# Six conditioning jobs moved out of the recurrence's tiles into the stage ahead of them

## The chip, the cores and the metric

The kernel runs on one core of a Trainium2 chip, as one program in which the instructions of each engine are written out in order and tied to one another by semaphores. The engines are TensorE (PE, matmuls into PSUM banks), VectorE (DVE), ScalarE (ACT), GpSimd (POOL) and SyncE (SP, which issues most of the DMAs). The metric is device time in microseconds: 1748.57 us, the median of three runs (1746.95 to 1749.58).

## The reference, cut to what matters

Two blocks are computed on 256 tokens of width 1024, all in fp32. The first begins with a conditioning: six vectors are made from `c`, and three of them (`g1`, `sh2`, `sc2`) are what this change moves.

```python
mod = silu(c) @ ada_w + ada_b                       # 1024 -> 6 * 1024
sh1, sc1, g1, sh2, sc2, g2 = split(mod, 6)
h = rms_norm(x, norm1_g) * (1 + sc1) + sh1
z = h @ w_in
y_fox = fox_mixer(z[..., :FOX_COLS], ...)           # attention, 8 heads
y_rwkv = rwkv7_mixer(z[..., FOX_COLS:], ...)        # recurrence, 8 heads
x = x + g1 * (concat([y_fox, y_rwkv]) @ w_out)
h = rms_norm(x, norm2_g) * (1 + sc2) + sh2
x = x + g2 * moe_ffn(h, ...)

# inside rwkv7_mixer
zr = zr + mu * (shift_prev(zr) - zr)                # token shift
w_log = -softplus(-(w0 + tanh(wd) @ decay_up)) - 0.5
a = sigmoid(a0 + ad @ iclr_up)
g = sigmoid(gd) @ gate_up
# per token: S = S * w + (S a) b^T + v k^T ; out = S r
```

A second block (another mixer, cross attention, a gated FFN) follows the experts; it isn't touched.

## The kernel before, in words

**Jobs.** A *job* is one dense product with 512 columns of a weight matrix. Its weights (2 MB, plus 2 KB of bias) are streamed by SyncE into one of two slots of `ring`, job by job in the order of the list `jobs`; the DMA of a job waits until the job two places before it is done (`w_used`, L670). `dense` and `dense_tile` (L1160 to L1186) do a job on TensorE: eight fp32 matmuls of 128x512 (the trace shows two records for each), one for the bias, and at the end a wait for the job's own last matmul. ScalarE copies the result out of its bank (`lin_copy`, L769; `side_copy`, L821). Results go to banks 0 and 1 in turn; `lin_bank` (L610) gives some outputs bank 2 or 3 instead.

**The conditioning jobs.** Each of the vectors takes two jobs (halves). The left operand is `silu_c`, which is ready from the start, so such a job depends only on its weights and may stand anywhere in TensorE's order. The six of this change are SHIFT2 (`sh2`), GATE1 (`g1`) and SCALE2 (`sc2`), in this order in the job list, after the projections and the `g2` jobs. They are used after the recurrence: `g1` where the output projection is added to `x` (L2233), `sc2` at L2225, `sh2` at L2257.

**The stages around them**, in TensorE's order:
1. Attention, eight heads; the projection of the recurrence and the two `g2` jobs stand between the heads. Meanwhile GpSimd does the token shift of `z_rw` in two halves (L1908 to L1919), each by a DMA and three operations.
2. ScalarE takes tanh and sigmoid of the low-rank columns of `z_rw` (L854 to L856) and signals `rw_tanh`.
3. TensorE transposes these columns (L1286) and does the low-rank products (L1292 to L1301); VectorE adds the biases, and ScalarE takes sigmoids (L859, L861).
4. VectorE makes the key norms (L2107 to L2115); ScalarE takes the square root (`rstd`, L862). Only then does VectorE scale `logw` (L2119), and TensorE makes the cumulative sums (L1303 to L1313). VectorE prepares the four operands `til` (L2121 to L2145).
5. The recurrence, two tiles of 128 tokens, each with: transposes of `til` (L1317), Gram products of each head (L1323 to L1326, L1331), an inverse by seven levels of doubling, and the end of the tile.

**A level** (L1340 to L1362) goes through two groups of four heads. For each group TensorE multiplies by `gram` (L1347), VectorE masks the result (L2174), TensorE multiplies twice more (L1356, L1360), and VectorE adds both results (L2179, L2181). The first level has no L1347, the last no L1360. In levels 1 to 4 a quarter of a job stands between L1347 and L1356: SHIFT2 in the first tile, SCALE2 in the second.

**The end of a tile**: products L1380, L1388, L1396 and L1398, with a copy by ScalarE after each group (L880 to L884). In the first tile the state's products follow (L1405, L1406), and VectorE makes `stateT` of them (L2189). There the two GATE1 jobs stand: the first in two halves between these products, the second behind them.

ScalarE needs a table load (`ACT_TABLE_LOAD`) where the function changes between the families of exp, square root, tanh and sigmoid. Copies need none.

Of the kernel before, what the change touches and what calls it, by code (L numbers as in the profile page):

```python
# [17 lines left out]
ALU = mybir.AluOpType  # L18
# [118 lines left out]
def build(nc, A, consts, out):  # L137
# [22 lines left out]
    with ctx:  # L160
# [25 lines left out]

        SH, SC, GT = range(3)


# [385 lines left out]
        J_IN2 = J_OUT + 2  # L575
        J_ADA2 = (J_SHIFT2, J_SCALE2)
        N_LATE = 4
# [32 lines left out]
        def lin_bank(o):  # L610


            return o % 2 + 2 * (o in [outputs[(j + i, 0)] for j in J_ADA2 for i in range(2)]
                                or o in [outputs[(J_OUT + 1, t)] for t in range(T)])

        def after(j, t=0):

            return outputs[(j, t)] + 1
# [122 lines left out]
        def _(act):  # L741
# [99 lines left out]
            for h in range(HEADS):  # L841
# [8 lines left out]
                if h < len(FOX_FILL):  # L850
                    side_copy(*FOX_FILL[h])
            rstd(fs[:, 6, 0:16], fs[:, 5, 0:16])

            act.wait_ge(lerp_done, 2)  # L854
            act.activation(z_rw[:, :, 1536:1600], z_rw[:, :, 1536:1600], ACT.Tanh)
            act.activation(z_rw[:, :, 1664:1824], z_rw[:, :, 1664:1824], ACT.Sigmoid).then_inc(rw_tanh, 1)  # L856
            for t in range(T):
                act.wait_ge(lora_in, 2 * t + 1)
                act.activation(logw[:, t, :], logw[:, t, :], ACT.Sigmoid).then_inc(rw_sig, 1)  # L859
                act.wait_ge(lora_in, 2 * t + 2)  # L860
                act.activation(iclr[:, t, :], iclr[:, t, :], ACT.Sigmoid).then_inc(rw_sig, 1)  # L861
            rstd(ws[:, 1, :], ws[:, 0, :])  # L862

# [10 lines left out]
            for t in range(T):  # L874

                side_copy(J_ADA2[t], 0)
                side_copy(J_ADA2[t] + 1, 0)

                act.wait_ge(u_mm, 3 * t + 1)
                act.activation(rhs_u[:, 0, :], bank[2][:, :], ACT.Copy).then_inc(u_evac, 1)  # L880
                act.wait_ge(u_mm, 3 * t + 2)
                act.activation(rhs_u[:, 1, :], bank[3][:, :], ACT.Copy).then_inc(u_evac, 1)
                act.wait_ge(u_mm, 3 * t + 3)
                act.activation(y_rw[:, t, :], bank[2][:, :], ACT.Copy).then_inc(u_evac, 1)  # L884
                if t == 0:
                    for h in range(2):
                        lin_copy(J_GATE1 + h, 0, tmp[:, h * BANK:(h + 1) * BANK])
            rstd(ws[:, 1, :], ws[:, 0, :])
# [265 lines left out]
        def _(pe):  # L1154
# [124 lines left out]
            for h in range(HEADS):  # L1279
# [4 lines left out]
                attend(h)  # L1284

            pe.wait_ge(rw_tanh, 1)  # L1286
            for t in range(T):
# [4 lines left out]
            for t in range(T):  # L1292
# [8 lines left out]
                    .then_inc(sc_mm, 1)  # L1301

            for t in range(T):  # L1303
                pe.wait_ge(logw_ready, t + 1)
                pe.matmul(score_bank()[:, :], cst["mid"][:, :], logw[:, t, :], start=True, stop=True)\
                    .then_inc(sc_mm, 1)
# [7 lines left out]
            for t in range(T):  # L1314
# [12 lines left out]
                for g in range(2):  # L1327
# [5 lines left out]
                    mm.then_inc(sc_mm, 1)  # L1333
                pe.wait_ge(lin_evac, after(J_GATE1 + 1 if t else J_GATE + 1))
                if t == 0:
                    pe.wait_ge(pv_evac, 1)
                else:
                    pe.wait_ge(u_evac, 3)

                for level in range(LEVELS):  # L1340
                    for g in range(2):
                        slots = range(4 * g, 4 * g + 4)
                        step = (LEVELS * t + level) * 2 + g
                        if level:
# [4 lines left out]
                            mm.then_inc(wkv_mm, 1)  # L1349
                        if 1 <= level <= 4:  # L1350

                            n = 2 * (level - 1) + g
                            dense_tile(J_ADA2[t] + n // 4, 0, cb, 1, True, part=(n % 4, 4))
                        pe.wait_ge(wkv_w, step + 1)
# [20 lines left out]

                pe.wait_ge(lin_evac, after(J_ADA2[t] + 1))
                with_state(bank[2], AT_)
# [4 lines left out]
                mm.then_inc(u_mm, 1)  # L1382
                if t == 0:
                    dense_tile(J_GATE1, 0, cb, 1, True, part=(0, 2))
                pe.wait_ge(u_evac, 3 * t + 1)
# [3 lines left out]
                mm.then_inc(u_mm, 1)  # L1389
                if t == 0:  # L1390
                    dense_tile(J_GATE1, 0, cb, 1, True, part=(1, 2))
                pe.wait_ge(u_evac, 3 * t + 2)
# [8 lines left out]
                if t == 0:  # L1401
                    b = score_bank()
                    for pair in range(4):
                        c = slice(pair * P, (pair + 1) * P)
                        pe.matmul(b[:, c], til[:, BT_, 0, c], rhs_u[:, 1, c], start=True, stop=False)  # L1405
                        mm = pe.matmul(b[:, c], til[:, KTT_, 0, c], z_rw[:, 0, 1024 + pair * P:1024 + (pair + 1) * P],  # L1406
                                       start=False, stop=True)
                    mm.then_inc(sc_mm, 1)
                    dense(J_GATE1 + 1, cb, 1, True)

# [518 lines left out]
        def _(dve):  # L1929
# [297 lines left out]
            for j in range(2):  # L2227
                for t in range(T):
                    o = outputs[(J_OUT + j, t)]
                    c = slice(j * BANK, (j + 1) * BANK)  # L2230
                    dve.wait_ge(lin_mm, o + 1)

                    dve.tensor_tensor(xn[:, t, c], bank[lin_bank(o)][:, :], tmp[:, c], ALU.mult).then_inc(lin_evac, 1)  # L2233
                    dve.wait_ge(lin_evac, o + 1)
                    link(dve.tensor_tensor(x[:, t, c], x[:, t, c], xn[:, t, c], ALU.add))
# [614 lines left out]
```

## Time and profile before

| | |
|---|---|
| median of three runs | 1748.57 us |
| lowest, highest | 1746.95, 1749.58 us |
| the profiled execution | 1751.06 us |
| its span, first to last instruction | 1749.2 us |
| mean granted TensorE clock | 0.890 |
| attention's end to the output projection | about 260 to 514 us of the span |

The page shows one execution. Busy times of TensorE's matmuls are modelled at their ends, and records overlap a little. `PEclk`, the granted clock, is a share of full speed: 1.00 is 2.4 GHz, 0.50 is 1.2 GHz, and means between come from stretches that hold both. In a timeline, the bracket at a row's end says how long the engine was idle before it, and what released it; `DVEq` or `POOLq` is the engine's own queue.

### The profile page before, as it was taken

How to read it: one execution, taken by the hardware profiler on the slowest of the kernel's cores; microseconds unless marked ns; L12 is line 12 of the kernel's file. 1: busy time of each engine (PE TensorE's matmuls, PEld its weight loads, DVE VectorE, ACT ScalarE, POOL GpSimd, SP SyncE). 2: the span in 40 equal slices, each digit the busy share in tenths (PEclk: the TensorE clock that was granted, in tenths of full speed). 3: DMA queues.
4: the chain of work that ended last, by engine and by line, in shares of the span. 5: the costliest groups of instructions: out<-in, count | busy, mean ns of one | idle time of the engine just before them, and what ended most of it. 6: DMA issues, size and time to landing. Idle time of an engine off the chain costs nothing.

```text
span 1749.2 us, 17988 instructions
## 1 busy us (share of the span) xinstructions
PE 1482.3 (85%) x6888; PEld 911.6 (52%) x6888; DVE 667.5 (38%) x1195; ACT 360.2 (21%) x605; POOL 34.8 (2%) x20
## 2 busy tenths in 40 slices
PE   6784984698987899999999999589978677599996
PEld 2342441666764444444444444366656436299974
DVE  1201527642454622222222222453355522457652
ACT  0010212000001112222222222134321111334342
POOL 0000032000000000000000000000000000000000
PEclk9888985699987899999999999789858887699998
DMA  7543170022119079999999998644321121145541
GB/s 266 194 153 111 45 217 1 1 97 97 51 47 377 16 316 420 415 421 416 408 420 415 414 414 353 230 133 144 82 63 48 49 96 48 48 145 169 169 169 72
DMA packets 106416, 338.98 MB, mean 194 GB/s; under 512 B 12455, under 2 KB 38474, under 8 KB 80636
## 3 DMA queue, kind: packets, MB, share of 16 engines
q1 hardware_dynamic: 93208, 319.09, 47.7%
q10 hardware_dynamic: 8500, 15.72, 3.2%
q0 software_dynamic: 4656, 3.44, 0.8%
q8 instruction: 37, 0.61, 0.1%
q14 instruction: 15, 0.12, 0.0%
HBM read 333.21 MB, written 1.05 MB: 191 GB/s over the span
## 4 chain that ended last, share of the span: by engine, by line
PE 74%; DVE 12%; another core or an unknown queue 4%; DMA 3%; issue 2%; ACT 2%; POOL 1%; ACTq 1%; DVEq 0%; SPq 0%; PEldq 0%; POOLq 0%
PE bank L1537 13%; PE bank L1171 12%; PE bank L1553 7%; PE bank L1190 5%; PE bank L1191 5%; PE bank L1192 5%; PE bank L1202 2%; PE bank L1500 2%; PE bank L1356 2%; PE bank L1501 2%; PE bank L1518 2%; PE bank L1520 2%; PE bank L1651 2%; DMA ring<-in_ada_b 1%
## 5 line engine op out<-in xcount | busy, mean ns | idle before, releaser
L1171 PE MATMUL bank<-ring,xT 128*128 128x512 f32 (+3 forms) x480 | 200.9, 574 | 18.4 <-DMA ring<-in_w_in 13.0
L1171 PEld LDWEIGHTS bank<-ring,xT 128*128 128x128 f32 x480 | 93.5, 210 | 116.7 <-issue 94.9
L1553 PE MATMUL bank<-dn,tmp 128*64 128x512 f32 x528 | 120.6, 598 | 0.0
L1190 PE MATMUL bank<-mod,w_high 128*128 128x256 f32 x352 | 100.9, 287 | 11.6 <-PE bank L1192 5.4
L1171 PE MATMUL bank<-ring,silu_c 128*128 128x512 f32 x192 | 91.2, 618 | 18.6 <-DMA ring<-in_ada_b 18.0
L2414 DVE TENSOR_TENSOR xT<-bank,mod 128x512 fp32r<-128x512 f32 x66 | 45.6, 692 | 158.0 <-ACT mod L948 150.7
L1191 PE MATMUL bank<-xT,w_high 128*128 128x256 f32 x352 | 99.1, 282 | 0.0
L1192 PE MATMUL bank<-mod,ring 128*128 128x256 f32 x352 | 98.8, 281 | 0.0
L2407 DVE SCALAR_TENSOR_TENSOR tmp<-silu_c,rc,bank 128x256 f32<-128x256 f32 x33 | 22.6, 684 | 196.7 <-ACT silu_c L935 191.4
L2777 DVE TENSOR_TENSOR ring<-ring,w_high 128x1024 fp32r<-128x1024 f32 x66 | 77.6, 1220 | 26.3 <-ACT w_high L1113 24.7
L1202 PE MATMUL bank<-c_ident,xn 128*128 128x128 f32 x120 | 28.3, 415 | 66.8 <-DVEq L2477 25.4
L1190 PEld LDWEIGHTS bank<-mod,w_high 128*128 128x128 f32 x352 | 67.3, 191 | 15.7 <-issue 15.7
L1113 ACT ACTIVATE w_high<-ring 128x1024 fp32r<-128x1024 f32 x66 | 65.8, 1049 | 30.5 <-DMA ring<-in_w_ffn_out 27.3
L1553 PEld LDWEIGHTS bank<-dn,tmp 128*64 128x64 f32 x528 | 35.0, 136 | 68.3 <-issue 68.3
L1500 PE MATMUL bank<-mod,gains 128*128 128x256 f32 x272 | 70.1, 296 | 0.5 <-ACT gains L916 0.5
L1191 PEld LDWEIGHTS bank<-xT,w_high 128*128 128x128 f32 x352 | 66.6, 189 | 0.0
L1171 PEld LDWEIGHTS bank<-ring,silu_c 128*128 128x128 f32 x192 | 36.4, 200 | 57.9 <-issue 50.8
L1192 PEld LDWEIGHTS bank<-mod,ring 128*128 128x128 f32 x352 | 66.6, 189 | 0.0
L1501 PE MATMUL bank<-mod,xn 128*128 128x256 f32 x272 | 66.3, 282 | 0.0
L948 ACT ACTIVATE mod<-bank 128x512 fp32r<-128x512 f32 x64 | 38.2, 597 | 133.8 <-PE bank L1553 133.8
L1500 PEld LDWEIGHTS bank<-mod,gains 128*128 128x128 f32 x272 | 51.5, 189 | 26.9 <-issue 26.2
L1537 PE MATMUL bank<-ring,gains 128*64 128x512 f32 x272 | 62.1, 598 | 1.4 <-ACT gains L922 1.4
(571 smaller groups left out, 2494.9 us busy)
## 6 DMA issues: line engine op xcount, KB each, us to landing
dn<-in_exp_w_down SPq DMA_DIRECT2D x66, 1024.0 KB, 10.5
ring<-in_exp_w_gate SPq DMA_DIRECT2D x34, 1024.0 KB, 9.5
ring<-in_exp_w_up SPq DMA_DIRECT2D x34, 1024.0 KB, 11.6
gu_odd<-in_exp_w_gate SPq DMA_DIRECT2D x32, 1024.0 KB, 10.2
gu_odd<-in_exp_w_up SPq DMA_DIRECT2D x32, 1024.0 KB, 12.3
ring<-in_ada_w SPq DMA_DIRECT2D x12, 2048.0 KB
ring<-in_w_ffn_in SPq DMA_DIRECT2D x22, 1024.0 KB, 5.1
ring<-in_w_in SPq DMA_DIRECT2D x7, 2048.0 KB
```

What stands on the lines that cost most here:

```text
L1113: act.activation(of_unit(w_high, u, q, PIECE), of_unit(ring, u, q, PIECE), ACT.Copy)\
L1171: mm = pe.matmul(bank[lin_bank(o)][:, 0:n], lhs(k, t), ring[:, j % RING, k * n:(k + 1) * n], start=(k == 0), stop=(k == kt - 1 and not bias))
L1190: pe.matmul(out, w[0], x[0], start=start, stop=False, skip_group_check=True)
L1191: pe.matmul(out, w[0], x[1], start=False, stop=False, skip_group_check=True)
L1192: return pe.matmul(out, w[1], x[0], start=False, stop=stop, skip_group_check=True)
L1202: mm = pe.transpose(bank[4 + n % 2][0:rows, lo:hi], src, cst["ident"][0:m, 0:m])
L1500: pe.matmul(out_k, xn_high[:, t, k * P:(k + 1) * P], pick[:, t, :], start=(t == 0), stop=False)
L1501: mm = pe.matmul(out_k, xn_low[:, t, k * P:(k + 1) * P], pick[:, t, :], start=False, stop=(t == T - 1))
L1537: mm = pe.matmul(bank[4][CHUNKS[c], :], hg_k[:, CHUNKS[c]], gate_up_of(gu_w(c), k), start=(k == 0), stop=(k == KT - 1))
L1553: mm = pe.matmul(bank[6 + h][CHUNKS[c], :], act_eT[:, 0, k, CHUNKS[c]], dn[:, 2 * parity + c, lo:lo + BANK], start=(k == 0), stop=(k == D_ ...
L2414: dve.tensor_tensor(y_low[:, c], bank[6 + h][:, :], y_high[:, c].bitcast(F32), ALU.subtract)\
L2777: dve.tensor_tensor(at_piece(w_low), at_piece(ring), at_piece(w_high).bitcast(F32), ALU.subtract)\
```

## The change

Six jobs leave the recurrence. The four of SHIFT2 and GATE1 now stand on TensorE between the attention and the low-rank transposes, and the two of SCALE2 between the low-rank products and the cumulative sums. On ScalarE their copies move too: four ahead of tanh, two ahead of the square root of the key norms. GATE1 is written to a free half of `gain` instead of `tmp`, which the attention still uses; the six jobs now take banks 0 and 1 only. The order of the jobs among themselves, and SyncE's order, stay as they are. The lines of the new kernel are numbered up to 8 off from the old ones.

```diff
+        gate1 = gain[:, 0, :]
...
-            return o % 2 + 2 * (o in [outputs[(j + i, 0)] for j in J_ADA2 for i in range(2)]
-                                or o in [outputs[(J_OUT + 1, t)] for t in range(T)])
+            return o % 2 + 2 * (o in [outputs[(J_OUT + 1, t)] for t in range(T)])
...   # ScalarE
             rstd(fs[:, 6, 0:16], fs[:, 5, 0:16])
+            for h in range(2):
+                side_copy(J_SHIFT2 + h, 0)
+            for h in range(2):
+                lin_copy(J_GATE1 + h, 0, gate1[:, h * BANK:(h + 1) * BANK])
             act.wait_ge(lerp_done, 2)
             act.activation(z_rw[:, :, 1536:1600], z_rw[:, :, 1536:1600], ACT.Tanh)
...
+            for h in range(2):
+                side_copy(J_SCALE2 + h, 0)
             rstd(ws[:, 1, :], ws[:, 0, :])
...
             for t in range(T):
-                side_copy(J_ADA2[t], 0)
-                side_copy(J_ADA2[t] + 1, 0)
...
-                if t == 0:
-                    for h in range(2):
-                        lin_copy(J_GATE1 + h, 0, tmp[:, h * BANK:(h + 1) * BANK])
...   # TensorE
+            for j in range(J_SHIFT2, J_SCALE2):
+                dense(j, cb, 1, True)
             pe.wait_ge(rw_tanh, 1)
...
+            for j in range(J_SCALE2, J_OUT):
+                dense(j, cb, 1, True)
             for t in range(T):
                 pe.wait_ge(logw_ready, t + 1)
...
-                        if 1 <= level <= 4:
-                            n = 2 * (level - 1) + g
-                            dense_tile(J_ADA2[t] + n // 4, 0, cb, 1, True, part=(n % 4, 4))
...
-                if t == 0:
-                    dense_tile(J_GATE1, 0, cb, 1, True, part=(0, 2))
...
-                if t == 0:
-                    dense_tile(J_GATE1, 0, cb, 1, True, part=(1, 2))
...
-                    dense(J_GATE1 + 1, cb, 1, True)
...   # VectorE
-                    dve.tensor_tensor(xn[:, t, c], bank[lin_bank(o)][:, :], tmp[:, c], ALU.mult)
+                    dve.tensor_tensor(xn[:, t, c], bank[lin_bank(o)][:, :], gate1[:, c], ALU.mult)
```

What this does to ScalarE's row of instructions ahead of tanh, before (`mod` and `gain` take the copies of the jobs, `z_rw` holds the low-rank columns, `fs` a small root of the attention):

```order
L767 ACTIVATE fs<-fs 128x16 [waits inv_var]
L855 ACT_TABLE_LOAD
L855 ACTIVATE z_rw<-z_rw 128x2x64 [waits lerp_done]
L856 ACT_TABLE_LOAD
L856 ACTIVATE z_rw<-z_rw 128x2x160
L859 ACTIVATE logw<-logw 128x512 [waits lora_in]
```

The same place in the changed kernel:

```order
L766 ACTIVATE fs<-fs 128x16 [waits inv_var]
L770 ACTIVATE mod<-bank 128x512 [waits lin_mm] x2
L770 ACTIVATE gain<-bank 128x512 [waits lin_mm] x2
L858 ACT_TABLE_LOAD
L858 ACTIVATE z_rw<-z_rw 128x2x64 [waits lerp_done]
L859 ACT_TABLE_LOAD
L859 ACTIVATE z_rw<-z_rw 128x2x160
L862 ACTIVATE logw<-logw 128x512 [waits lora_in]
```

Four copies, each waiting for a job's end, now stand ahead of the table load of tanh.

ScalarE's row between the sigmoids of the second tile and the exponentials of the cumulative sums, before (`ws` is the root of the key norms):

```order
L859 ACTIVATE logw<-logw 128x512 [waits lora_in]
L861 ACTIVATE iclr<-iclr 128x512 [waits lora_in]
L767 ACT_TABLE_LOAD
L767 ACTIVATE ws<-ws 128x16 [waits inv_var]
L866 ACT_TABLE_LOAD
L866 ACTIVATE rhs_u<-bank 128x512 [waits sc_mm]
```

And in the changed kernel:

```order
L862 ACTIVATE logw<-logw 128x512 [waits lora_in]
L864 ACTIVATE iclr<-iclr 128x512 [waits lora_in]
L770 ACTIVATE mod<-bank 128x512 [waits lin_mm] x2
L766 ACT_TABLE_LOAD
L766 ACTIVATE ws<-ws 128x16 [waits inv_var]
L871 ACT_TABLE_LOAD
L871 ACTIVATE rhs_u<-bank 128x512 [waits sc_mm]
```

The two copies of SCALE2 and, behind them, a table load now stand ahead of the root.

TensorE's row in a level of the first tile, one group of heads, before:

```order
L1347 MATMUL bank<-inv,gram 128x128 [waits wkv_upd]
L1347 MATMUL bank<-inv,gram 128x128 x3
L1171 MATMUL bank<-ring,silu_c 128x512 [waits lin_evac,w_full1]
L1171 MATMUL bank<-ring,silu_c 128x512
L1356 MATMUL bank<-invT,amat 128x128 [waits wkv_w]
L1356 MATMUL bank<-invT,amat 128x128 x3
L1360 MATMUL bank<-amat,invT 128x128 x4
```

And in the changed kernel:

```order
L1350 MATMUL bank<-inv,gram 128x128 [waits wkv_upd]
L1350 MATMUL bank<-inv,gram 128x128 x3
L1355 MATMUL bank<-invT,amat 128x128 [waits wkv_w]
L1355 MATMUL bank<-invT,amat 128x128 x3
L1359 MATMUL bank<-amat,invT 128x128 x4
```

The quarter of a job is gone from between the product by `gram` and the product that waits for VectorE's mask (`wkv_w`).

## Rows read from the trace of the kernel before

**Rows 1.** The page, part 1: busy us (share of the span) and instructions, by engine.

```profile
PE 1482.3 (85%) x6888; PEld 911.6 (52%) x6888; DVE 667.5 (38%) x1195; ACT 360.2 (21%) x605; POOL 34.8 (2%) x20
```

**Rows 2.** Timeline, 256 to 282: start, us, engine, line, operation, [idle before <-releaser].

```profile
259.57 0.63 PE L1275 MATMUL bank<-z_fox,xn 128*128 128x64 f32 x2
...
268.36 1.28 ACT L855 ACT_TABLE_LOAD   x1
...
276.38 0.31 ACT L855 ACTIVATE z_rw<-z_rw 128x128 f32<-128x128 f32 x1 [6.74 <-POOLq L1919]
...
278.51 1.54 PE L1202 MATMUL bank<-c_ident,z_rw 128*128 128x128 f32 x6 [18.31 <-ACT z_rw L856]
```

**Rows 3.** Timeline, 290 to 302, VectorE and ScalarE.

```profile
294.94 0.69 DVE L2102 COPY gate<-bank 128x512 f32<-128x512 f32 x1 [3.29 <-PE bank L1300]
...
300.38 0.22 ACT L767 ACTIVATE ws<-ws 128x16 f32<-128x16 f32 x1 [6.62 <-DVE ws L2113]
...
300.63 1.00 DVE L2119 TENSOR_SCALAR logw<-logw 128x512 f32<-128x512 f32 x2 [0.28 <-ACT ws L767]
```

**Rows 4.** Timeline, TensorE: one job alone, and 32 records from 513.86.

```profile
415.01 7.03 PE L1171 MATMUL bank<-ring,silu_c 128*128 128x512 f32 x16
...
423.13 0.60 ACT L771 ACTIVATE tmp<-bank 128x512 f32<-128x512 f32 x1 [8.67 <-PE bank L1176]
...
423.40 1.07 PE L1202 MATMUL bank<-c_ident,til 128*128 128x128 f32 x8 [0.30 <-PE bank L1176]
...
513.86 16.73 PE L1171 MATMUL bank<-ring,xT 128*128 128x512 f32 x32 [0.78 <-DVE xT L1954]
```

**Rows 5.** SyncE's issue of a job's weights, and the stretch after it (columns as rows 8).

```profile
361.55 0.37 SPq L673 DMA_DIRECT2D ring<-in_ada_w  x1
...
361.50:369.50 8.00, 7.92 (x54) 6.60 (x55) 2.55 (x4) 0.56 (x1) 0.00 (x0) 1.00 0.75 261
```

**Rows 6.** Timeline of the first tile's levels: products of the first and fifth to seventh.

```profile
343.59 1.89 PE L1347 MATMUL bank<-inv,gram 128*128 128x128 f32 x8
...
382.46 1.06 PE L1347 MATMUL bank<-inv,gram 128*128 128x128 f32 x8
...
384.84 1.16 PE L1356 MATMUL bank<-invT,amat 128*128 128x128 f32 x8 [1.32 <-DVE amat L2174]
...
390.46 1.06 PE L1347 MATMUL bank<-inv,gram 128*128 128x128 f32 x8
```

**Rows 7.** Timeline of TensorE at the end of each tile.

```profile
397.67 2.00 PE L1380 MATMUL bank<-z_rw,gram 128*128 128x64 f32 x16 [0.84 <-DVEq L2183]
...
409.58 0.41 PE L1396 MATMUL bank<-rhs_u,gram 128*128 128x64 f32 x2
...
413.17 0.44 PE L1405 MATMUL bank<-rhs_u,til 128*128 128x128 f32 x2
...
497.31 1.90 PE L1380 MATMUL bank<-z_rw,gram 128*128 128x64 f32 x16
...
499.89 2.00 PE L1388 MATMUL bank<-rhs_u,invT 128*128 128x64 f32 x16 [0.69 <-ACT rhs_u L880]
```

**Rows 8.** Stretches: their us, busy us by engine (instructions), granted clock, DMA share, GB/s.

```profile
280.00:296.00 16.00, 13.13 (x17) 3.52 (x16) 5.44 (x11) 3.80 (x5) 0.00 (x0) 0.50 0.00 0
304.00:312.00 8.00, 0.71 (x2) 0.00 (x0) 7.62 (x12) 0.37 (x1) 0.00 (x0) 0.71 0.00 0
325.54:337.48 11.94, 11.71 (x76) 11.52 (x77) 5.44 (x9) 0.00 (x0) 0.00 (x0) 0.61 0.00 0
...
384.00:396.00 12.00, 8.27 (x67) 7.70 (x67) 5.62 (x9) 0.00 (x0) 0.00 (x0) 1.00 0.33 125
426.85:435.80 8.95, 8.16 (x77) 7.40 (x78) 5.15 (x8) 0.00 (x0) 0.00 (x0) 1.00 0.41 154
498.00:502.00 4.00, 3.21 (x27) 2.93 (x26) 1.38 (x2) 0.67 (x2) 0.00 (x0) 1.00 0.02 4
504.45:511.17 6.72, 6.72 (x34) 6.72 (x33) 0.00 (x0) 0.00 (x0) 0.00 (x0) 0.50 0.00 0
```

More of the change, by code:

```diff
@@ L575, in build @@
         J_IN2 = J_OUT + 2
-        J_ADA2 = (J_SHIFT2, J_SCALE2)
         N_LATE = 4
@@ L1333, in _ @@
                     mm.then_inc(sc_mm, 1)
-                pe.wait_ge(lin_evac, after(J_GATE1 + 1 if t else J_GATE + 1))
                 if t == 0:
+                    pe.wait_ge(lin_evac, after(J_SCALE2 + 1))
                     pe.wait_ge(pv_evac, 1)
@@ L1374, in with_state @@
                                   start=(pair == 0), stop=False, skip_group_check=True)
-                pe.wait_ge(lin_evac, after(J_ADA2[t] + 1))
                 with_state(bank[2], AT_)
@@ L2231, in _ @@
                     dve.wait_ge(lin_mm, o + 1)
-                    dve.tensor_tensor(xn[:, t, c], bank[lin_bank(o)][:, :], tmp[:, c], ALU.mult).then_inc(lin_evac, 1)
+                    dve.tensor_tensor(xn[:, t, c], bank[lin_bank(o)][:, :], gate1[:, c], ALU.mult).then_inc(lin_evac, 1)
                     dve.wait_ge(lin_evac, o + 1)
```

## The prediction

> **What bounds the kernel now.** I read the page's list of busy times first: TensorE is busy 85% of the span [rows 1], so it sets the time on average. That says nothing about one stage, so I then read the timeline of 256 to 530 us, where all six jobs run before and after the change, and last the granted clock by stretches. In the stage ahead of the recurrence TensorE is not the bound. It ends the attention at 259.57 + 0.63 = 260.20 us and starts the low-rank transposes at 278.51, 18.31 us later, released by ScalarE's sigmoid, which itself ran as soon as GpSimd's token shift was done [rows 2]. After the low-rank products VectorE works alone: its gate copy starts at 294.94, ScalarE gives it the square root at 300.38, and at 300.63 it scales logw for the cumulative sums [rows 3]. In the recurrence TensorE is full as long as it carries pieces of the jobs; in the levels without them it waits for VectorE [rows 6].
>
> **One job.** GATE1's second half runs unbroken at full clock: its matmuls start at 415.01, ScalarE's copy at 423.13 (8.12 us), the next work at 423.40, so a job costs 8.39 us on TensorE while others follow [rows 4]. A burst that starts at half clock pays more: the 32 records from 513.86 last 16.73 us, against 2 x 7.03 = 14.06 for as many at full clock, so about 2.7; I take 3.0, since the job's bias pair is not among them. The weights of a job (2 MB) are issued when the job two places before is done. The load of 361.55 is over inside the 8 us to 369.5, where the engines moved 261 GB/s, 2.1 MB in all [rows 5]. A job lasts 8.39 us, so back-to-back jobs just find their weights. This cover is thin: 1 us more per load would cost up to 1 us at each of the last two jobs of the first group.
>
> **The first group** (SHIFT2, GATE1: four jobs, ahead of the transposes). TensorE: 3 x 8.39 + 8.12 + 3.0 for the half-clock start = 36.3 us. Now the point that decides. ScalarE's four copies stand ahead of its tanh, and the table load of tanh stands behind them (the order rows of the section on the change show it). Before, that load ran at 268.36 under the wait for GpSimd and cost nothing; the step from tanh's start to the transposes was 278.51 - 276.38 = 2.13 us [rows 2]. After, the last copy (0.60), the load (1.28) and that step (2.13) follow the last job: 4.0 us. So the transposes start at 260.20 + 36.3 + 4.0 = 300.5 instead of 278.51: **+22.0 us**. The idle 18.31 us hides two jobs and a little; GpSimd's shift, done by 276.4, is no longer what ends last. Queued behind the waiting tanh are the sigmoids, and for these TensorE, VectorE's loraT copies and everything later. The low-rank products ran at granted clock 0.50 (280 to 296) [rows 8]. TensorE will sit idle for the 4.0 us before them. In 304 to 312, where it is busy for only 0.71 of 8 us, the mean clock is 0.71: it was full in some part and was lost within the stretch [rows 8]. So I give them nothing back: 0, bounds -6.5 (half of their 13.13 busy us) and 0.
>
> **The second group** (SCALE2: two jobs, ahead of the cumulative sums). TensorE: 8.39 + 8.12 + 3.0 = 19.5 us from 294.94 on the old time scale. The sums themselves were needed late, so behind TensorE alone most of this would hide under VectorE's work. But ScalarE's two copies stand ahead of its square root of the key norms, with the table load behind them again, and VectorE waits for that root before it scales logw. So VectorE goes on at 294.94 + 19.5 + 0.60 + 1.28 + 0.25 (300.38 to 300.63) = 316.5 instead of 300.63: **+15.9 us**, on the path, since all that VectorE prepares for the recurrence comes after that wait. The weights are there: they are issued as the GATE1 jobs end.
>
> Sum of costs: 37.9 us. Its bounds are 31 (the low-rank products give back their 6.5) and 43 (loads late, clock slow to rise: some 5 more).
>
> **What the recurrence gives back.** Four levels with pieces take 382.46 - 343.59 = 38.87 us in the first tile. The level after them, without a piece, takes 390.46 - 382.46 = 8.00, and in it TensorE waits 1.32 us for VectorE's mask product [rows 6]. So four bare levels take 32.0, and I add 0.5 because the first products run at half clock. Gain 6.4 a tile, **12.8 us** for both, though the four jobs are 4 x 8.12 = 32.5 us of TensorE time: the rest was already lying in VectorE's shadow. The clock stayed 1.00 in 384 to 396, almost the whole of it bare levels [rows 8], so I expect it to stay there.
>
> End of the first tile: from 397.67 to 423.40 are 25.73 us [rows 7, 4]. Without GATE1 the chain is: first product and ScalarE's copy, 2.58 us (497.31 to 499.89, where the second tile has no filler); the inverse's product and copy, as much; the output products, 413.17 - 409.58 = 3.59; the state's products, 415.01 - 413.17 = 1.84; and 1.0 because VectorE makes the state before it can copy the next transposes. Together 11.6, a gain of 14.1. But in the second tile, where these steps already stand bare, the clock is 1.00 in 498 to 502 and 0.50 in 504.45 to 511.17, and the same output products last 6.72 us [rows 8]. I expect the same in the first tile now: 6.72 for 3.59, 3.68 for 1.84, less 0.5 as VectorE's state is then less late: 16.1, a gain of 9.6. And the second tile's Gram stage, now 8.95 us at 1.00, then goes like the first tile's, 11.94 us at 0.61: 3.0 back. Net **6.6 us**; bounds 6.6 and 14.1.
>
> Here a rule speaks for the change. The Trainium skill (TensorE: Matmul & The Clock Gate, "Why this matters for your kernels") asks for no idle gaps over about 3 us between bursts of matmuls. The gaps here are under 1 us, so by that rule the clock would hold at the end of the tile, and the gain there would be 14.1; the rows of 498 to 511 do not bear it out. It is the first rival.
>
> Another page would make it dearer: the Trainium skill (ScalarE: Activation LUTs, "What ACT_TABLE_LOAD costs") counts a drain of 1.38 us beside each load's 1.28. By it the two loads laid open would add 2.8 us. The trace disagrees: tanh, a load and the sigmoid fit in 2.13 us, so the sum stays.
>
> **Sum.** 22.0 + 15.9 - 12.8 - 6.6 = **+18.5 us**. Against the profiled execution's span of 1749.2 us that is 1767.7, and with the 1.9 us around its span (1751.06 in all) 1769.6; the median of the runs shown, 1748.57, lies 2.5 below that execution, so I forecast **1767 us**. The stages behind only shift: the output projection finds its weights earlier than now, but it never waited for them.
>
> **Rivals.**
> - *The clock holds at the end of the first tile.* Gain there 14.1 instead of 6.6: +11.0, 1759.6 us. For it: small gaps; the clock was 1.00 through all of 384 to 396. Against: the second tile's rows. 15%.
> - *The clock holds everywhere, the change is no slower.* With the long idle stretch filled, TensorE keeps full clock from the first group through the low-rank products and the second group to the Gram products. To the rival above add 6.5 (low-rank products), 3.0 (no second half-clock start), 3.0 (the first Gram stage like the second) and 0.5: +11.0 - 13.0 = -2.0, 1746.6 us. It decides if the clock survives the 4.0 us wait for tanh. Against it stands that it was lost inside 304 to 312. 6%.
> - *VectorE is no bound in the levels.* If bare levels shrank by the jobs' whole time, the levels would give 32.5 instead of 12.8: -1.2, 1747.4 us. The bare level's 8.00 us and its waits stand in the trace, so 2%.
> - *The bare levels lose the clock.* The wide matmuls could be what holds it: 504 to 511 shows that TensorE can be busy 100% and stay at 0.50. TensorE is busy 8.27 of the 12 us from 384 to 396, so 5.5 of a level's 8; at half clock that is 11, and a level about 12 us. For eight levels and the four last ones that is about +47, in all +65, 1814 us; for a part of them +10 to +20 more than forecast. Against: 384 to 396. 7% for all of these.
>
> **Chances and range.** The forecast's own case 70%, with its own range 1760 to 1775: the half-clock starts (1.5 to 5 us each), the loads (up to 2), the tile end. The rest as above. A measurement of this kernel tells 0.2% (3.5 us) from no change. Slower 0.90 (forecast, first rival and lost clock make 0.92; 0.02 goes to what I have not thought of), same 0.05 and faster 0.05 from the second and third rivals, whose times lie close to today's, and that rest. The range 1755 to 1778 holds the forecast's case and the first rival.
>
> **What would show it.** Right: in the profile after, no idle TensorE from 260 to about 296, then some 4 us of it, with tanh's table load inside; transposes near 300; VectorE idle for about 16 us before it scales logw, released by ScalarE's square root, which follows a copy and a table load; levels of 8.0 us in both tiles; the output products of the first tile near 6.7 us at clock 0.50. Wrong: transposes before 295, VectorE not waiting for the root, or levels under 7 us would break the sum; levels of 10 us or more mean that the clock fell there.

## The result and the profile after

| | before | after |
|---|---|---|
| median | 1748.5 us (4 runs, 1746.95 to 1749.58) | 1769.13 us (4 runs, 1766.54 to 1772.84) |
| the profiled execution | 1751.06 us | 1766.78 us |
| its span | 1749.2 us | 1764.9 us |
| mean granted clock | 0.890 | 0.892 |

The ratio of after to before is 1.012, with a 95% interval from 1.0096 to 1.0144: the changed kernel is slower by 20.6 us in the medians. The forecast was 1767 us.

Page of the kernel after, part 1: busy us (share of the span) and instructions, by engine. It answers to [rows 1].

```profile
PE 1493.7 (85%) x6888; PEld 919.1 (52%) x6888; DVE 668.5 (38%) x1195; ACT 360.3 (20%) x605; POOL 34.8 (2%) x20
```

Each engine has as many instructions as before, and the shares hardly moved. Nothing here tells that the kernel became slower, or where; only the timeline does.

Timeline of after, 260 to 302, TensorE (to be read against [rows 2]; columns as there):

```profile
260.95 8.60 PE L1170 MATMUL bank<-ring,silu_c 128*128 128x512 f32 x16
...
270.90 7.10 PE L1170 MATMUL bank<-ring,silu_c 128*128 128x512 f32 x16 [0.30 <-PE bank L1175]
...
287.82 7.10 PE L1170 MATMUL bank<-ring,silu_c 128*128 128x512 f32 x16 [0.30 <-PE bank L1175]
294.85 1.12 PE L1175 MATMUL bank<-ring,ones 1*128 1x512 f32 x2
300.05 1.54 PE L1201 MATMUL bank<-c_ident,z_rw 128*128 128x128 f32 x6 [4.08 <-ACT z_rw L859]
```

And ScalarE in the same stretch:

```profile
296.01 0.60 ACT L770 ACTIVATE gain<-bank 128x512 f32<-128x512 f32 x1 [7.86 <-PE bank L1175]
296.63 1.28 ACT L858 ACT_TABLE_LOAD   x1
297.92 0.31 ACT L858 ACTIVATE z_rw<-z_rw 128x128 f32<-128x128 f32 x1
298.24 1.28 ACT L859 ACT_TABLE_LOAD   x1
299.53 0.47 ACT L859 ACTIVATE z_rw<-z_rw 128x320 f32<-128x320 f32 x1
```

The first group of jobs fills TensorE without a gap for weights (0.30 us between jobs), and the idle time of 18.31 us has become 4.08 us: a copy, a load, tanh, a load, the sigmoid, one behind the other. The transposes start at 300.05 instead of 278.51.

VectorE of after, 316 to 339, around its wait for the root (answers to [rows 3]):

```profile
316.26 0.69 DVE L2095 COPY gate<-bank 128x512 f32<-128x512 f32 x1 [3.29 <-PE bank L1301]
...
321.41 0.25 DVE L2106 RECIPROCAL ws<-ws 128x16 f32<-128x16 f32 x1
337.88 1.00 DVE L2112 TENSOR_SCALAR logw<-logw 128x512 f32<-128x512 f32 x2 [16.22 <-ACT ws L766]
```

ScalarE of after, the work that VectorE waits for:

```profile
327.27 0.60 ACT L770 ACTIVATE mod<-bank 128x512 f32<-128x512 f32 x1 [13.48 <-PE bank L1175]
335.73 0.60 ACT L770 ACTIVATE mod<-bank 128x512 f32<-128x512 f32 x1 [7.86 <-PE bank L1175]
336.34 1.28 ACT L766 ACT_TABLE_LOAD   x1
337.63 0.22 ACT L766 ACTIVATE ws<-ws 128x16 f32<-128x16 f32 x1
```

And TensorE's first SCALE2 job, the longest start of a group in any of the traces (7.03 us at full clock):

```profile
316.15 10.03 PE L1170 MATMUL bank<-ring,silu_c 128*128 128x512 f32 x16
```

VectorE had the input of the root ready at 321.66 and got it at 337.85. The root is 0.22 us of work; what made it late is what stands in front of it on ScalarE.

TensorE of after in the first tile: a bare level, and its end (answers to [rows 6, 7]):

```profile
390.37 1.06 PE L1350 MATMUL bank<-inv,gram 128*128 128x128 f32 x8
392.75 1.16 PE L1355 MATMUL bank<-invT,amat 128*128 128x128 f32 x8 [1.32 <-DVE amat L2167]
...
398.37 1.06 PE L1350 MATMUL bank<-inv,gram 128*128 128x128 f32 x8
...
429.57 2.00 PE L1378 MATMUL bank<-z_rw,gram 128*128 128x64 f32 x16 [0.84 <-DVEq L2176]
432.25 2.00 PE L1384 MATMUL bank<-rhs_u,invT 128*128 128x64 f32 x16 [0.69 <-ACT rhs_u L882]
434.94 0.69 PE L1390 MATMUL bank<-rhs_u,gram 128*128 128x64 f32 x2 [0.69 <-ACT rhs_u L884]
...
441.82 0.74 PE L1399 MATMUL bank<-rhs_u,til 128*128 128x128 f32 x2
...
445.13 1.04 PE L1201 MATMUL bank<-c_ident,til 128*128 128x128 f32 x8
```

The first bare level of the second tile, which began slowly:

```profile
464.93 1.91 PE L1350 MATMUL bank<-inv,gram 128*128 128x128 f32 x8
...
475.41 1.06 PE L1350 MATMUL bank<-inv,gram 128*128 128x128 f32 x8
```

Stretches of after: their us, busy us by engine (instructions), granted clock, DMA share, GB/s.

```profile
300.05:316.20 16.15, 14.60 (x23) 4.57 (x23) 4.64 (x9) 2.52 (x4) 0.00 (x0) 0.50 0.20 77
...
362.80:375.20 12.40, 12.40 (x68) 12.18 (x69) 5.53 (x8) 0.00 (x0) 0.00 (x0) 0.50 0.00 0
384.00:428.00 44.00, 31.93 (x259) 29.84 (x260) 21.16 (x33) 0.00 (x0) 0.00 (x0) 1.00 0.00 1
434.94:441.82 6.88, 6.88 (x33) 6.88 (x33) 0.00 (x0) 0.00 (x0) 0.00 (x0) 0.50 0.00 0
448.80:457.60 8.80, 7.25 (x67) 6.24 (x65) 5.60 (x10) 0.00 (x0) 0.00 (x0) 1.00 0.01 2
461.00:471.00 10.00, 8.34 (x40) 7.81 (x41) 3.83 (x6) 0.00 (x0) 0.00 (x0) 0.55 0.00 0
472.00:512.00 40.00, 29.29 (x238) 27.20 (x236) 19.43 (x31) 0.00 (x0) 0.00 (x0) 1.00 0.00 1
```

A bare level (one without a piece of a job) is 8.00 us, 390.37 to 398.37, with the same 1.32 us wait for VectorE as before the change. The bare levels kept full clock for 44 us with TensorE busy 73% (31.93 of 44). The output products that follow, without any idle time, ran at 0.50. The second tile shows what the prediction did not foresee: its Gram products kept 1.00, and its levels began near 0.5, so that the first took 10.48 us (464.93 to 475.41).

### The profile page after: what moved, and what is told of

Same layout as the page of the kernel before. It is cut to its first block, busy times and chain, and to the rows that moved or that the text cites. A ratio compares the mean times of both kernels' runs of the same rounds, so it can differ in the third digit from the quotient of the medians.

```text
span 1764.9 us, 17987 instructions
## 1 busy us (share of the span) xinstructions
PE 1493.7 (85%) x6888; PEld 919.1 (52%) x6888; DVE 668.5 (38%) x1195; ACT 360.3 (20%) x605; POOL 34.8 (2%) x20
## 4 chain that ended last, share of the span: by engine, by line
PE 75%; DVE 14%; another core or an unknown queue 4%; issue 2%; ACT 2%; DMA 1%; ACTq 1%; DVEq 0%; SPq 0%; PEldq 0%
PE bank L1530 13%; PE bank L1170 13%; PE bank L1546 7%; PE bank L1189 5%; PE bank L1191 5%; PE bank L1190 5%; PE bank L1201 2%; PE bank L1493 2%; PE bank L1355 2%; PE bank L1494 2%; PE bank L1511 2%; PE bank L1513 2%; PE bank L1644 2%; DMA ring<-in_ada_b 1%
## 5 line engine op out<-in xcount | busy, mean ns | idle before, releaser
L1170 PE MATMUL bank<-ring,xT 128*128 128x512 f32 (+3 forms) x480 | 198.7, 569 | 18.3 <-DMA ring<-in_w_in 12.7
L1170 PE MATMUL bank<-ring,silu_c 128*128 128x512 f32 x192 | 94.1, 647 | 19.3 <-DMA ring<-in_ada_b 17.6
## 6 DMA issues: line engine op xcount, KB each, us to landing
dn<-in_exp_w_down SPq DMA_DIRECT2D x66, 1024.0 KB, 10.4
```

The lines of the kernel that those rows point to most:

```text
L1170: mm = pe.matmul(bank[lin_bank(o)][:, 0:n], lhs(k, t), ring[:, j % RING, k * n:(k + 1) * n], start=(k == 0), stop=(k == kt - 1 and not bias))
```

## The experiments

The theory: **ScalarE's order is the price**. The jobs lie in cover, that is in time in which TensorE would wait anyway (for GpSimd's shift, for VectorE's preparations), or are paid back; what is lost is that tanh and the root, short steps that others wait for, stand behind copies that wait for whole jobs. The rival, **the jobs themselves**: TensorE's time ahead of the transposes and sums costs what it costs, wherever the copies stand. Each kernel below was timed beside the kernel before, on the same chip. The first four comparisons share 28 runs of it (median 1750.2) on one chip, the last four 18 (median 1748.01) on another. So a kernel is judged by how far it lies above or below the kernel before of its own comparison: the change is 20.6 us above by the first measurement and 20.5 by its repeat. Of the medians forecast below, three came out 0.3 to 0.8 us under their ranges, and the last two single figures were missed by 2 to 3 us. Lengths between two events of one trace are used where attention ended at different times.

**The root ahead of the SCALE2 copies** (in the kernel after):

```diff
+            rstd(ws[:, 1, :], ws[:, 0, :])
             for h in range(2):
                 side_copy(J_SCALE2 + h, 0)
-            rstd(ws[:, 1, :], ws[:, 0, :])
```

> The changed kernel, with ScalarE's two SCALE2 copies moved behind its square root of the key norms; TensorE's order is untouched. Theory A (ScalarE's order makes the price of the second group): VectorE no longer waits 16.2 us for the root. Its preparation then meets the cumulative sums, which still stand behind the two jobs: about 10 us less than the changed kernel, some 1759 us. Rival B (the two jobs on TensorE ahead of the sums are the price by themselves): the sums can start only about 2.7 us earlier, so 0 to 3 us less, 1766 to 1769 us.

Measured: 1758.85 us (1750.05 to 1762.82, 12 runs), ratio 1.0045 [1.0029 to 1.0061]. It lies 8.7 us above the kernel before instead of 20.6, so 12 us are gone by moving one line. Timeline of this kernel, ScalarE:

```profile
318.32 1.28 ACT L766 ACT_TABLE_LOAD   x1
326.22 0.22 ACT L766 ACTIVATE ws<-ws 128x16 f32<-128x16 f32 x1 [6.62 <-DVE ws L2106]
330.61 0.60 ACT L770 ACTIVATE mod<-bank 128x512 f32<-128x512 f32 x1 [4.17 <-PE bank L1175]
```

And VectorE:

```profile
326.46 1.00 DVE L2112 TENSOR_SCALAR logw<-logw 128x512 f32<-128x512 f32 x2 [0.28 <-ACT ws L766]
...
342.17 0.69 DVE L2130 TENSOR_TENSOR y_rw<-bank,logw 128x512 f32<-128x512 f32 x1 [4.43 <-ACT rhs_u L872]
```

The table load is back under the wait for VectorE, and logw follows the root at once, as before the change. Not all 15.9 us come back: the cumulative sums still stand behind both jobs (339.33 here), and VectorE is idle 4.43 us for them. From the gate copy to the transposes of `til`, where before needs 25.94 us and after 41.87, this kernel needs 30.34 (320.77 to 351.11). So 4.4 us of the second group's price are left with TensorE's order, and 11.5 went with ScalarE's. About 1 us of the 11.5 is the clock: the first of the two jobs took 8.85 us here and 10.03 in after. Against the repeat of after (40.47 us, first job 8.64) it is 10.1.

**Tanh and sigmoid ahead of the first four copies**:

```diff
-            for h in range(2):
-                side_copy(J_SHIFT2 + h, 0)
-            for h in range(2):
-                lin_copy(J_GATE1 + h, 0, gate1[:, h * BANK:(h + 1) * BANK])
             act.wait_ge(lerp_done, 2)
...          # tanh, sigmoid
+            for h in range(2):
+                side_copy(J_SHIFT2 + h, 0)
+            for h in range(2):
+                lin_copy(J_GATE1 + h, 0, gate1[:, h * BANK:(h + 1) * BANK])
```

> The changed kernel, with the four copies of the first group moved behind tanh and sigmoid. The third job then waits for a copy (some 2.5 us), but the 4.1 us idle time of TensorE ahead of the transposes goes. Theory A: 1.5 us less if the clock is lost again before the low-rank products, 8 us less if it holds through them (they run at 0.50 in the changed kernel), 1761 to 1767 us. Rival B (the jobs' own time is all the price): no gain or slower by the 2.5 us.

Measured: 1761.95 us (1760.79 to 1762.95, 6 runs), ratio 1.0069 [1.0050 to 1.0088], 11.7 us above the kernel before instead of 20.6. Timeline of this kernel, TensorE, from the third job to the low-rank products:

```profile
279.79 8.51 PE L1170 MATMUL bank<-ring,silu_c 128*128 128x512 f32 x16 [2.28 <-ACT mod L770]
...
296.69 1.12 PE L1175 MATMUL bank<-ring,ones 1*128 1x512 f32 x2
298.12 0.84 PE L1201 MATMUL bank<-c_ident,z_rw 128*128 128x128 f32 x6 [0.30 <-PE bank L1175]
...
302.86 2.08 PE L1300 MATMUL bank<-gate_up,loraT 128*128 128x512 f32 x2 [0.81 <-DVEq L2088]
```

And stretches of this kernel:

```profile
297.00:299.00 2.00, 1.66 (x8) 0.58 (x6) 0.26 (x1) 0.60 (x1) 0.00 (x0) 1.00 0.02 2
300.00:314.00 14.00, 13.19 (x17) 3.70 (x18) 3.56 (x6) 2.52 (x4) 0.00 (x0) 0.50 0.36 139
```

In this trace the condition of the prediction's second rival (that the clock survives) fails even without the wait. TensorE comes to the transposes at full clock, without the idle 4 us, and does them in 0.84 us instead of 1.54; the low-rank products behind them run at 0.50 all the same. The time from the transposes' start to the gate copy is 15.78 us (298.12 to 313.90) against 16.21 in after. So here it was not the gap that took the clock; the last section shows an execution in which it held for most of this stage.

The gain in the medians is 8.9 us. The traces locate less: from attention's end to the transposes behind the recurrence it is 4.0 against after (268.35 to 264.37) and 1.8 against the repeat of after (266.17). Of the 4.0, only 0.7 lie ahead of the transposes, since the third job now waits 2.28 us for its bank behind the copies that wait behind the sigmoid; 0.4 are in the low-rank products, 1.4 in the second group, whose first job took 8.60 us instead of 10.03, and 1.4 in the first tile. Theory A gave 1.5 us for a clock that is lost, as it was here, so the median stands in its range by luck, and most of this gain has no place in a trace.

**Both edits together**:

> Both orders of the two runs before in one kernel. Theory A: the sum of the two, 12 to 18 us less than the changed kernel, 1751 to 1757 us, close to the kernel before with all six jobs still in the stage ahead. Rival B: 0 to 3 us less.

Measured: 1750.52 us (1741.69 to 1756.49, 12 runs), ratio 0.9992 [0.9972 to 1.0012]. TensorE's third job, and VectorE behind the root:

```profile
281.02 7.11 PE L1170 MATMUL bank<-ring,silu_c 128*128 128x512 f32 x16 [0.44 <-ACT mod L770]
...
319.00 1.00 DVE L2112 TENSOR_SCALAR logw<-logw 128x512 f32<-128x512 f32 x2 [0.28 <-ACT ws L766]
```

With the six jobs where the change put them, and only ScalarE's order mended, the kernel can't be told from the one before: 0.3 us above it instead of 20.6. The two edits alone give 12.0 and 8.9. The rival is refuted as an explanation of the loss. In the traces the stretch from attention's end to the transposes behind the recurrence falls from 268.35 to 250.77 us (before: 250.96). Of these 17.6 us, 3.1 lie ahead of the low-rank transposes, where attention ended 2.2 us later than in the trace of tanh and sigmoid alone and the third job waits only 0.44 us; 11.2 lie in the second group. The other 3.3 stand where no edit was made: 2.3 in the second tile, whose four bare levels took 31.4 us instead of 34.5 because the clock held, and 1.0 in the low-rank products and the first tile. What stays true of the rival: the jobs' time on TensorE (17.5 us more ahead of the transposes, 4.7 more in the second group) is about what the recurrence gives back (21.4), so the move as such gains nothing.

**SCALE2 back in the second tile's levels**, the other four jobs as in after:

```diff
-            for j in range(J_SCALE2, J_OUT):
-                dense(j, cb, 1, True)
...
+                        if t and 1 <= level <= 4:
+                            n = 2 * (level - 1) + g
+                            dense_tile(J_SCALE2 + n // 4, 0, cb, 1, True, part=(n % 4, 4))
```

> The changed kernel with the SCALE2 pair back in the second tile's levels 1 to 4; SHIFT2 and GATE1 stay in the first group. Theory A: the second group's 15.8 us go, and the levels of the second tile give back 5 to 7 us, since there the jobs lie mostly in VectorE's shadow: 9 to 11 us less than the changed kernel, 1758 to 1760 us. Rival B (a job costs TensorE's time wherever it stands): no difference.

Measured: 1757.69 us (1749.92 to 1760.5, 11 runs), ratio 1.0032 [1.0015 to 1.0049]. The logw scaling follows the gate copy by 5.7 us again (315.88, 321.56), and the four levels with pieces take 40.0 us (447.48 to 487.49) against 34.5 in after (464.93 to 499.39). It lies 7.5 us above the kernel before instead of 20.6, so 13.1 are gone. In the traces the second group gives 15.9 and the levels take 5.6, 10.4 net; by the prediction's terms it was 15.9 - 6.4 = 9.5. That a job costs its time wherever it stands is refuted.

**The kernel after, once more**, for its scatter:

> The changed kernel itself, timed beside the next three on one chip: 1.2% above the kernel before by the first measurement (1769 against 1748.5 us). Both theories expect that again; it is the base for the others.

Measured: 1768.53 us (1762.1 to 1772.57, 6 runs), ratio 1.0115 [1.0094 to 1.0136]. The profiled execution shows the same events: transposes at 299.88 after 4.08 us of idle time, VectorE's wait for the root 14.83 us instead of 16.22, because the first SCALE2 job took 8.64 us and not 10.03. The second group cost 14.5 us here (40.47 less 25.94), not 15.9. The second tile's levels again began slowly, 461.95 to 468.23 for the first group of heads, as in after (464.93 to 471.20). The four levels took 34.5 us in four of the five traces that have them bare in the second tile; only in that of both edits, 31.4.

**Only SHIFT2 moved into the gap**, from the kernel before, its copies behind the sigmoid. GATE1 keeps its place in this run and the next, but is written to `gain` as in after:

```diff
             act.activation(z_rw[:, :, 1664:1824], z_rw[:, :, 1664:1824], ACT.Sigmoid).then_inc(rw_tanh, 1)
+            for h in range(2):
+                side_copy(J_SHIFT2 + h, 0)
...
+            for j in range(J_SHIFT2, J_GATE1):
+                dense(j, cb, 1, True)
             pe.wait_ge(rw_tanh, 1)
...
-                        if 1 <= level <= 4:
+                        if t and 1 <= level <= 4:
```

> The kernel before with only the SHIFT2 pair moved, to the place between attention and low-rank transposes, its copies behind tanh and sigmoid. Theory A: two jobs take 19.5 us from the attention's end, 18.3 of which TensorE idles through anyway, so +1.3 us; the first tile's levels give back 6.9. In sum some 5.5 us less than the kernel before, about 1743 to 1745 us. Rival B (levels cannot give back anything since VectorE bounds them, or a moved job costs its time): 1749 us or more.

Measured: 1742.19 us (1736.7 to 1747.51, 12 runs), ratio 0.9961 [0.9947 to 0.9975]. Timeline of this kernel, TensorE:

```profile
260.44 8.92 PE L1172 MATMUL bank<-ring,silu_c 128*128 128x512 f32 x16
...
270.72 7.10 PE L1172 MATMUL bank<-ring,silu_c 128*128 128x512 f32 x16 [0.30 <-PE bank L1177]
277.76 1.12 PE L1177 MATMUL bank<-ring,ones 1*128 1x512 f32 x2
279.18 0.85 PE L1203 MATMUL bank<-c_ident,z_rw 128*128 128x128 f32 x6 [0.30 <-ACT z_rw L856]
```

Attention ends at 260.65 here and the transposes start 18.5 us later, against 18.3 in before: two jobs lie wholly in the wait for GpSimd, whose end they just reach. The first tile's four levels shrink to 32.2 us (341.08 to 373.28), from 38.87. So the bare levels of a tile are worth what the prediction said, and whether a job's move wins depends on the cover at the place where it goes and on what waits behind its copies. The stretch from attention's end to the transposes behind the recurrence is 9.8 us shorter in this trace (250.96 to 241.19), more than the 5.8 of the medians: 3.0 of it is the first Gram stage (22.71 to 19.72), which ran at 0.94 here.

**Only SHIFT2 moved ahead of the sums**, its copies ahead of the root. The matmuls stand before the wait for `logw_ready`:

```diff
+            for h in range(2):
+                side_copy(J_SHIFT2 + h, 0)
             rstd(ws[:, 1, :], ws[:, 0, :])
...
+            for j in range(J_SHIFT2, J_GATE1):
+                dense(j, cb, 1, True)
             for t in range(T):
                 pe.wait_ge(logw_ready, t + 1)
```

> The kernel before with only the SHIFT2 pair moved, to the place ahead of the cumulative sums, its copies ahead of the square root as in the changed kernel's second group. It measures that group's price alone. Theory A: +15.9 us, less 6.9 from the first tile's levels: +9, about 1758 us. Rival B (the price is hidden under VectorE's preparation, as the sums are needed 11 us later than they are made): no change or up to 5 us less, 1744 to 1749 us.

Measured: 1755.25 us (1751.27 to 1758.3, 7 runs), ratio 1.0036 [1.0023 to 1.0049]. VectorE of this kernel, which waits 15.28 us for the root:

```profile
314.87 1.00 DVE L2123 TENSOR_SCALAR logw<-logw 128x512 f32<-128x512 f32 x2 [15.28 <-ACT ws L767]
```

It lies 7.2 us above the kernel before; the same two jobs that save 6 us in the gap cost 7 here. From the gate copy (294.18) to the transposes of `til` (335.11) are 40.93 us, 15.0 more than before. The second group's price is a property of this place and of ScalarE's order, not of what stands ahead of it. This run doesn't separate the two; the first experiment does (4.4 us for the place, the rest for the order).

**Each pair where it finds cover**: SHIFT2 in the gap as above; GATE1 behind the cumulative sums, with its copies behind the exponentials; SCALE2 left in the second tile.

```diff
+            for j in range(J_GATE1, J_SCALE2):      # TensorE, behind the cumulative sums
+                dense(j, cb, 1, True)
...          # ScalarE, behind the exponentials of the cumulative sums
+            for h in range(2):
+                lin_copy(J_GATE1 + h, 0, gate1[:, h * BANK:(h + 1) * BANK])
```

> A version built from the findings. SHIFT2 stands between attention and low-rank transposes, its copies behind the sigmoid (+1.3 us); GATE1 stands behind the cumulative sums, under VectorE's preparation, its copies behind the exponentials (two jobs of 19.5 us in about 16 us of idle TensorE, and the small state products behind them: +4 to +6); SCALE2 stays in the second tile's levels as before. The first tile's levels give back 6.9, its end about 10. Theory A: some 10 us less than the kernel before, about 1739 us. Rival B: 1748 us or more.

Measured: 1741.06 us (1735.29 to 1741.69, 5 runs), ratio 0.9954 [0.9940 to 0.9968]: faster than before by 7 us and than the repeat of after by 27. Its interval overlaps that of SHIFT2 alone, so what GATE1's move adds isn't shown. TensorE of this kernel:

```profile
304.21 7.09 PE L1171 MATMUL bank<-ring,silu_c 128*128 128x512 f32 x16
...
312.74 7.11 PE L1171 MATMUL bank<-ring,silu_c 128*128 128x512 f32 x16 [0.39 <-PE bank L1176]
...
322.83 1.07 PE L1202 MATMUL bank<-c_ident,til 128*128 128x128 f32 x8
```

Both GATE1 jobs run at full clock while VectorE prepares `til`; in before, TensorE was busy for 0.71 us of 304 to 312 [rows 8]. That is the cover which the change passed by: it put two jobs a few instructions earlier, ahead of the sums on which VectorE's work depends, instead of behind them.

## Why the prediction was right

The prediction's sum, term by term, against the two traces. Attention ended 0.96 us later in the profile of after, which is taken out.

| term | predicted | measured | from |
|---|---|---|---|
| first group | +22.0 | +20.6 | transposes 278.51 to 300.05, less 0.96 |
| low-rank products | 0 | -0.2 | 16.43 to 16.21, transposes to gate copy |
| second group | +15.9 | +15.9 | gate copy to transposes of `til`, 25.94 to 41.87 |
| first tile's Gram stage | 0 | +1.6 | 22.71 to 24.30 |
| its levels 1 to 4 | -6.4 | -6.9 | 38.87 to 31.93 |
| its end | -9.6 | -10.2 | 25.73 to 15.56 |
| second tile's Gram stage | +3.0 | +1.3 | 18.51 to 19.80 |
| its levels 1 to 4 | -6.4 | -4.7 | 39.20 to 34.46 |
| sum | +18.5 | +17.4 | rounded; attention's end to the transposes behind the recurrence |

With the 0.96 us ahead of it and 2.6 fewer behind it, the span grew by 15.7; the medians grew by 20.6. The two profiled executions differ from their medians in opposite directions (2.6 us above, 2.4 below), which is the 5 us between; no trace locates them. In the repeat of after the same stretch grew by 15.2 us instead of 17.4. So the terms stand to within 1 or 2 us, and that the sum meets the median to 2 us is in part luck.

- *First group.* Right in mechanism and place. The half-clock start was too dear: the first job took 8.60 us instead of 7.03, so 1.6 and not 3.0; over the eight traces with a job there it was 1.2 to 2.8. The 4.0 us behind the last job were there.
- *The drain of a table switch.* The Trainium skill (ScalarE: Activation LUTs, "What ACT_TABLE_LOAD costs") would have put 1.38 us beside each load. In the rows of after the last copy ends at 296.61, the load begins at 296.63, and tanh at 297.92; there is no room for it, as the prediction took it.
- *Second group.* Right in mechanism: moving the root alone took 10 to 11.5 of the 15.9 away. That it is right to 0.1 us is luck. It needs a start at half clock of 3.0 us, and this execution had it (10.03 us for the first job); the five other traces with jobs at this place had 1.6 to 2.1.
- *Levels.* 8.00 us each, VectorE's wait in them unchanged, so the third rival is refuted. The fourth, that bare levels lose the clock, came true for one level of the second tile (10.48 us) and for no other. The first tile gave 6.9.
- *First tile's end.* The output products took 6.88 us at 0.50 where 6.72 were expected, with the engine never idle: the first rival is refuted. The Trainium skill (TensorE: Matmul & The Clock Gate, "Why this matters for your kernels") asks for no idle gaps over about 3 us between bursts of matmuls, to avoid drops. No gap was that long here, and the clock fell all the same: from the first bare level to these products no gap was over 1.32 us, and the last two were 0.69 us.
- *Second tile.* This step was mis-sized. The prediction let its Gram stage fall to half clock (+3.0) and its levels be bare at full clock (-6.4). The clock did the reverse: 1.00 from 448.80 to 457.60, and 0.55 from 461 to 471, so that the first level took 10.48 us. The Gram stage lost 1.3 because VectorE, busy with the state, was late with `tilT` (TensorE idle 1.66 us at 447.83). Together 3.4 were predicted and 3.4 measured: two errors that cancel, and not a hit. In the trace of both edits the clock held through these levels (31.4 us), so this part is not fixed by the instructions either.
- *First Gram stage.* Not in the sum: it ran at 0.50 throughout (362.80 to 375.20) instead of 0.61, for 1.6 us. In the repeat of after the stage took 22.88 us, 0.2 more than before.

What stays open: why the same bare Gram and level products keep the clock in one place and lose it in another, and the larger part of the 8.9 us of the second experiment, which no trace locates. That ScalarE's order is the price is shown by the medians; which of its waits carry it is shown in the traces for the second group (10 to 11.5 us) and only in part for the first (0.7 to 3.1).

## What to carry to other kernels

A filler (a job put where its engine would be idle) is free only if its consumer's queue is free too: where it moves, look at which short step on the copying engine (here tanh, and a root of 0.22 us) comes to stand behind its copies, and on whether the table load stays under a wait. Put fillers behind the last instruction that another engine's long stretch depends on, not ahead of it; two jobs ahead of the sums cost 4.4 us even with the root in front of their copies. Place and copy order together made the same two jobs save 6 us in one gap and cost 7 in the next. Taking fillers out of a loop pays back only what was not already in another engine's shadow: 6.9 us for two jobs that take 16 us of TensorE.

## What the runs showed of the hardware

The granted clock did not follow how busy TensorE was. It was 1.00 for 44 us of levels at 73% busy, and 0.50 in output products at 100% (434.94 to 441.82) and in low-rank products at 90% (300.05 to 316.20, 14.60 of 16.15 us). Nor is it a property of the instructions. The last experiment and SHIFT2 alone have the same instructions on TensorE up to the cumulative sums, but not the same clock in the low-rank stage. The stretch of SHIFT2 alone:

```profile
279.00:295.00 16.00, 13.53 (x22) 4.11 (x22) 5.80 (x11) 4.72 (x7) 0.00 (x0) 0.57 0.37 132
```

And of the kernel with three places:

```profile
283.00:294.00 11.00, 9.18 (x21) 2.50 (x18) 4.60 (x9) 3.81 (x5) 0.00 (x0) 0.85 0.55 192
```

From the transposes to the gate copy the one took 16.25 us, the other 11.82. Attention ended 4 us apart in these two executions. So 4.4 us in this stage can come and go between executions. The three kernels that are not slower than before scatter by 6 to 15 us between their fastest and slowest runs (5 to 12 runs each), the kernel before by 9.5 in 18 and 11 in 28. In the kernel with both edits the shortest of the twelve runs had the highest mean clock (1741.69 us, 0.904) and the three longest 0.890 to 0.894. A single trace is no proof of a gain of this size.
